# A walk over chunk states placed between the first score maxima of an attention stage, and a last layer mixed from its first latent tile

## The chip, the cores and the metric

The kernel runs on one core of a Trainium2 chip. The metric is the time of one execution in microseconds, measured on the device; before the change it is 6207.06 us, the median of 3 runs (6197.98 to 6211.08). A core has five engines, each with its own instruction queue, that meet only in semaphores: TensorE (PE, matmuls into PSUM; PEld are its weight loads), VectorE (DVE), ScalarE (ACT), GpSimd (POOL) and SyncE (SP, which here only issues DMAs). PSUM has eight banks of 512 float32 columns.

## The reference

Two layers over 2304 tokens of width 1024: 256 context tokens and 2048 latent ones. Each layer projects to the inputs of four groups of heads and sums what they give through one output projection.

```python
def hybrid_layer(x, ctx, ..., ctx_out):
    h_lat = rmsnorm(x, norm_g) * (1.0 + scale[:, None]) + shift[:, None]
    h_ctx = rmsnorm(ctx, norm_g) * (1.0 + scale_c) + shift_c
    s_lat = split_cols(h_lat @ w_in)
    s_ctx = split_cols(h_ctx @ w_in)
    branches = (mlstm_branch(...), diff_attn_branch(...), ssd_branch(...), hgrn2_branch(...))
    y_lat = jnp.concatenate([br[0] for br in branches], axis=-1) @ w_out
    x = x + gate[:, None] * y_lat
...
def bidirectional(run, ctx_fwd, lat_fwd, ctx_bwd, lat_bwd, s0, ctx_out):
    yc_f, sc_f = run(ctx_fwd, s0, ctx_out)
    yl_f, _ = run(lat_fwd, sc_f, True)
    yc_b, sc_b = run(flip(ctx_bwd), s0, ctx_out)
    yl_b, _ = run(flip(lat_bwd), sc_b, True)
...
def chunk_state_scan(decay, incr, s0):
    def step(s, inp):
        d, u = inp
        return d * s + u, s
...
def diff_attend(q, k, v, lam):
    s = jnp.einsum('bqhmd,bkhmd->bhmqk', q, k).astype(F32) * (DA_QK ** -0.5)
    p = jax.nn.softmax(s, axis=-1)
    w = p[:, :, 0] - lam * p[:, :, 1]
    return jnp.einsum('bhqk,bkhv->bqhv', w, v)
```

Three of the four groups (mLSTM, SSD, HGRN2) are linear recurrences in both directions: over chunks a state is decayed and an increment of keys and values added, the context first, then the latent tokens. The fourth is differential softmax attention with its two maps for each of four heads. In the last layer nothing is given out for context tokens (`ctx_out` is false).

## The kernel before

The 2304 tokens are 18 tiles of 128, tiles 0 and 1 the context. The program is a row of stages, and each stage is a block that ends in a barrier of all engines (`k.clear`, with the semaphores cleared). A layer is projection, `gates`, `states`, `mixing`, `attention`, `output`.

`states` walks over the tiles in the order of the backward direction (1, 0, 17, ..., 3, so 17 steps) and writes for each tile the state at which it begins (`k.st`), a tile of 128 x 514: mLSTM, HGRN2, SSD. For a step, SP loads six pieces of the tile into one of four sets of buffers; TensorE makes the running sums of HGRN2's log decays (L1254, L1256), ACT their exponentials (L1235, L1236), VectorE the scaled key (L1183), GpSimd two more scaled operands (L1170, L1171), TensorE the increments (L1266 to L1273), and VectorE new state = decay x old state + increment (L1196 to L1206, reading PSUM). ACT's queue stores the state.

`mixing` goes through the 18 tiles forwards. It makes and keeps the forward state itself and loads the backward one from `k.st`. Its eight sub-steps a tile bind TensorE, ACT, VectorE and GpSimd closely together.

`attention` holds the queries and keys of all tiles, transposed (`QK`), in SBUF, and goes through the queries in groups of four tiles and two halves of heads. The softmax needs each row's maximum first. While one half's probabilities are made, the maxima of the next are made beside them; only for the first half is nothing there to hide them, and they stand by themselves at the start: 40 jobs (`prologue`), each one pair of score matmuls on TensorE (L2295) into one of three pairs of PSUM banks (`PRO`) and one VectorE reduction (L2148), with the key transposes (L2285) between them as the keys are needed. Then `maxima(0)` (L2141) gives the shift, GpSimd cuts it into pieces (`pieces(0)`), and the main loop starts.

All orders are the orders in which the code emits instructions; there is no scheduler. A wait holds up everything behind it on its engine. `Turns` keeps for each PSUM bank a list of the jobs that use it: `take` waits until the job before it in that bank was released.

Of the kernel before, what the change touches and what calls it, by code (L numbers as in the profile page):

```python
# [26 lines left out]
P = 128  # L27
# [8 lines left out]
H = 4  # L36
# [1029 lines left out]
class Turns:  # L1066


    def __init__(self, k, c, uses):
# [5 lines left out]
        self.full = {b: k.sem(c, f"bank{b}_full") for b in self.count}  # L1075
        self.free = {b: k.sem(c, f"bank{b}_free") for b in self.count}
# [29 lines left out]
def states(k, l):  # L1106

    nc = k.nc
    d = 1
    TILES = [*range(CT - 1, -1, -1), *range(NT - 1, CT - 1, -1)]  # L1110
    IN, RING, NLOAD = 4, 4, 6
    with ExitStack() as c:
        key = [k.sb(c, f"key{b}", [P, 256]) for b in range(IN)]
        va = [k.sb(c, f"va{b}", [P, H, 65]) for b in range(IN)]
        fi = [k.sb(c, f"fi{b}", [P, 512]) for b in range(IN)]
        kk = [k.sb(c, f"kk{b}", [P, 256]) for b in range(IN)]
        gt = [k.sb(c, f"gt{b}", [P, GW]) for b in range(IN)]
        xb = [k.sb(c, f"xb{b}", [P, 512]) for b in range(IN)]
        eh = [k.sb(c, f"eh{b}", [P, 256]) for b in range(2)]
        gh = [k.sb(c, f"gh{b}", [P, 2]) for b in range(2)]  # L1120
        kp = [k.sb(c, f"kp{b}", [P, 256]) for b in range(2)]
        xw = [k.sb(c, f"xw{b}", [P, 256]) for b in range(2)]
        kh = [k.sb(c, f"kh{b}", [P, 256]) for b in range(2)]
        S = [k.sb(c, f"S{b}", [P, STW]) for b in range(RING)]
        ones = k.sb(c, "ones", [P, 1])
        tri = k.sb(c, "tri", [P, 4, P])
        s = k.sems(c, "consts_in memsets exps_done weighted keyed updated "
                      + " ".join(f"in{b}" for b in range(IN)) + " " + " ".join(f"st_stored{b}" for b in range(RING)))
        steps = range(NT - 1)
        bk = Turns(k, c, [(("sum", n), n % 2) for n in steps] + [(("ml_hg", n), 2 + n % 2) for n in steps]  # L1130
                   + [(("ss", n), 4 + n % 2) for n in steps])
        h4 = lambda a: a.rearrange("p (h w) -> p h w", h=H)

        def loaded(eng, n):
            eng.wait_ge(s[f"in{n % IN}"], 16 * NLOAD * (n // IN + 1))

        with nc.Block() as block:
            @block.sync
            def _(sp):
                sp.dma_start(tri[:], k.x["c_tri"]).then_inc(s["consts_in"], 16)  # L1140
                sp.wait_ge(s["memsets"], 1)
                for n in steps:
                    b, u = n % IN, k.u[TILES[n]]
                    if n >= IN:
                        bk.wait(sp, ("ml_hg", n - IN))
                        bk.wait(sp, ("ss", n - IN))
                        sp.wait_ge(s["weighted"], n - IN + 1)
                        sp.wait_ge(s["updated"], n - IN + 1)
                    for o, i in ((fi[b][:], u[:, OFF["hg_f"] + 256:OFF["hg_f"] + 768]),
                                 (gt[b][:], k.gt[TILES[n]]),  # L1150
                                 (key[b][:], u[:, 256:512]),
                                 (xb[b][:], k.xc[TILES[n], :, 0:512]),
                                 (kk[b][:], u[:, OFF["hg_k"] + 256:OFF["hg_k"] + 512]),
                                 (va[b][:, :, 0:64], u[:, 512:768].rearrange("p (h w) -> p h w", h=H))):
                        sp.dma_start(o, i).then_inc(s[f"in{b}"], 16)

            @block.gpsimd
            def _(gp):
                gp.memset(ones[:], 1.0)
                for b in range(IN):  # L1160
                    gp.memset(va[b][:, :, 64:65], 1.0)
                gp.memset(S[0][:], 0.0).then_inc(s["memsets"], 1)
                for n in steps:
                    b = n % IN
                    g = lambda name: gt[b][:, GC[name] + 4 * d:GC[name] + 4 * d + 4].unsqueeze(2).to_broadcast([P, H, DH])
                    loaded(gp, n)
                    if n >= 2:
                        bk.wait(gp, ("ml_hg", n - 2))
                        bk.wait(gp, ("ss", n - 2))
                    nc.gpsimd.tensor_tensor(h4(kp[n % 2][:]), h4(key[b][:]), g("wk"), ALU.mult)  # L1170
                    nc.gpsimd.tensor_tensor(h4(xw[n % 2][:]), h4(xb[b][:, 0:256]), g("ws"), ALU.mult) \  # L1171
                        .then_inc(s["weighted"], 1)

            @block.vector
            def _(dve):
                V = nc.vector

                def keyed(n):
                    loaded(dve, n)
                    dve.wait_ge(s["exps_done"], n + 1)  # L1180
                    if n >= 2:
                        bk.wait(dve, ("ml_hg", n - 2))
                    V.tensor_tensor(kh[n % 2][:], kk[n % IN][:], eh[n % 2][:], ALU.mult).then_inc(s["keyed"], 1)  # L1183

                def update(n):
                    old, new, g = S[n % RING], S[(n + 1) % RING], gt[n % IN]
                    if n:
                        dve.wait_ge(s["updated"], n)
                    if n + 1 >= RING:
                        dve.wait_ge(s[f"st_stored{(n + 1) % RING}"], 16 * ((n + 1) // RING))  # L1190
                    bk.wait(dve, ("ml_hg", n))
                    inc = bk[("ml_hg", n)]
                    for p in range(2):
                        sl = slice(p * 65, p * 65 + 65)
                        a = GC["as"] + 2 * d + p
                        V.scalar_tensor_tensor(new[:, sl], old[:, sl], g[:, a:a + 1], inc[:, sl], ALU.mult, ALU.add)  # L1196
                        sl = slice(ST_HG + p * 64, ST_HG + p * 64 + 64)
                        ins = V.scalar_tensor_tensor(new[:, sl], old[:, sl], gh[n % 2][:, p:p + 1], inc[:, sl],
                                                     ALU.mult, ALU.add)
                    bk.release(ins, ("ml_hg", n))  # L1200
                    bk.wait(dve, ("ss", n))
                    inc = bk[("ss", n)]
                    for h in range(H):
                        sl = slice(ST_SS + h * 64, ST_SS + h * 64 + 64)
                        a = GC["ea"] + 4 * d + h
                        ins = V.scalar_tensor_tensor(new[:, sl], old[:, sl], g[:, a:a + 1], inc[:, h * 64:h * 64 + 64],  # L1206
                                                     ALU.mult, ALU.add)
                    bk.release(ins, ("ss", n))
                    bk.freed(dve, ("ss", n))
                    dve.sem_inc(s["updated"], 1)  # L1210

                dve.wait_ge(s["memsets"], 1)
                for n in steps:
                    keyed(n)
                    if n:
                        update(n - 1)
                update(NT - 2)

            @block.scalar
            def _(act):  # L1220
                act.preload_act_table_set(TABLES)

                def store(n):
                    if n:
                        act.wait_ge(s["updated"], n)
                    act.dma_start(k.st[TILES[n]], S[n % RING][:]).then_inc(s[f"st_stored{n % RING}"], 16)

                act.wait_ge(s["memsets"], 1)
                for n in steps:
                    bk.wait(act, ("sum", n))  # L1230
                    if n >= 2:
                        act.wait_ge(s["keyed"], n - 1)
                        act.wait_ge(s["updated"], n - 1)
                    b = bk[("sum", n)]
                    nc.scalar.activation(eh[n % 2][:], b[:, 0:256], ACT.Exp)  # L1235
                    bk.release(nc.scalar.activation(gh[n % 2][:], b[:, 256:258], ACT.Exp), ("sum", n))  # L1236
                    bk.freed(act, ("sum", n))
                    act.sem_inc(s["exps_done"], 1)
                    if n >= 1:
                        store(n - 1)  # L1240
# [1365 lines left out]
```

## Time and profile before

| | |
|---|---|
| median of 3 runs | 6207.06 us |
| the profiled execution: time, span | 6209.43 us, 6207.8 us |
| mean granted clock of TensorE | 0.939 |
| busy: PE, DVE, ACT, POOL | 89%, 47%, 27%, 38% |
| `states`, layer 0 and layer 1 | 87.65 us, 87.07 us |
| start of `attention` to the first shift, both layers | 60.69 us, 60.97 us |

The span runs from the first to the last instruction. Timelines give for a line its start, its duration, the engine, the line of the code, what it writes and reads, how many such instructions are merged (xN), and in brackets how long the engine had been idle and what released it. `SPq` and `ACTq` are DMA issues. The duration of a DMA issue is that of the issue, not of the transfer. The borders in the last two rows are read from the first GpSimd memset of a stage to that of the next, and to the reduction L2141.

### The profile page before, as it was taken

To read this page: it belongs to the slowest core of one execution; us is meant where nothing else is said; L and a number is where in the kernel's file an instruction comes from. 1 tells how busy PE (TensorE), PEld (TensorE's weight loads), DVE (VectorE), ACT (ScalarE), POOL (GpSimd) and SP (SyncE) were. 2 spreads that over 40 slices of the span, in tenths; PEclk is the share of its full clock that TensorE was granted. 3 is DMA by queue.
4 is the path that set the end of the run, shared out by engine and by line. 5 is a ranking of instruction groups with operands and counts; after the bars stand their busy time and mean duration, and the time that the engine had idled before them with its cause. 6 is when DMAs were issued, how large, how long until landed. Compare 5 with 4: busy or idle time off the path is not lost. (4 is left out here: it accounts for less than half of the span.)

```text
span 6207.8 us, 76211 instructions
## 1 busy us (share of the span) xinstructions
PE 5515.7 (89%) x26532; PEld 2933.7 (47%) x26532; DVE 2911.4 (47%) x5007; ACT 1697.7 (27%) x4109; POOL 2329.4 (38%) x1718
## 2 busy tenths in 40 slices
PE   3999999967888799997979999998588877999979
PEld 1444444446666433332435454544466663333334
DVE  0354444444666555551114545455365665555312
ACT  0112111112333234444012121211133332444421
POOL 0111212123333279997001212112233332999920
PEclk7999999977999889998989999999599997999989
DMA  8223233245222100001523333333622211000032
GB/s 293 76 98 103 97 103 100 95 144 160 77 75 91 62 1 8 8 6 53 207 105 103 99 100 101 101 101 108 188 94 74 78 56 56 1 8 8 4 115 88
DMA packets 382933, 534.46 MB, mean 86 GB/s; under 512 B 114784, under 2 KB 263344, under 8 KB 375964
## 3 DMA queue, kind: packets, MB, share of 16 engines
q1 hardware_dynamic: 356124, 455.81, 22.4%
q10 hardware_dynamic: 20448, 41.46, 1.7%
q0 software_dynamic: 6048, 33.11, 1.5%
q8 instruction: 185, 3.03, 0.2%
q14 instruction: 128, 1.05, 0.1%
HBM read 374.82 MB, written 155.13 MB: 85 GB/s over the span
## 5 line engine op out<-in xcount | busy, mean ns | idle before, releaser
L586 PE MATMUL psum<-group_W,projection_hT 128*128 128x512 f32 (+4 forms) x5016 | 1952.7, 546 | 5.9 <-DVE projection_hT L699 5.7
L586 PEld LDWEIGHTS psum<-group_W,projection_hT 128*128 128x128 f32 x5016 | 951.1, 191 | 970.6 <-issue 929.8
L2113 POOL TENSOR_TENSOR attention_PS<-attention_PS 128x1024 f32<-128x1024 f32 x548 | 1265.6, 2354 | 82.0 <-ACT attention_PS L2246 74.7
L2159 DVE TENSOR_REDUCE attention_mxp<-psum 128x1 f32<-128x512 f32 (+1 forms) x1016 | 654.7, 686 | 541.5 <-PE psum L2295 541.5
L2246 ACT ACTIVATE attention_PS<-psum 128x512 f32<-128x512 f32 (+1 forms) x1168 | 630.6, 592 | 717.8 <-PE psum L2349 695.2
L441 POOL TENSOR_TENSOR projection_cx<-projection_cx,projection_cw 128x768 f32<-128x768 f32 x102 | 187.6, 1840 | 1686.9 <-DMA projection_cw<-in_ss_conv_w 1686.9
L2295 PE MATMUL psum<-attention_QK 32*128 32x512 f32 (+1 forms) x2592 | 771.0, 609 | 9.1 <-DVE attention_mxp L2148 6.1
L2343 PE MATMUL psum<-attention_QK 32*128 32x512 f32 x2336 | 665.1, 643 | 0.0
L2361 PE MATMUL psum<-attention_PS,attention_va 128*64 128x512 f32 x2336 | 628.1, 616 | 0.0
L650 ACT ACTIVATE projection_ut<-psum 128x256 f32<-128x256 f32 (+2 forms) x322 | 127.3, 406 | 1420.5 <-PE psum L586 1411.5
L2479 PE MATMUL psum<-output_W,output_yT 128*128 128x512 f32 x1088 | 476.9, 597 | 21.0 <-DMA output_W<-in_w_out 21.0
L752 DVE TENSOR_SCALAR projection_e<-projection_e 128x256 f32<-128x256 f32 (+1 forms) x170 | 58.8, 346 | 849.9 <-ACT projection_e L662 849.8
L2343 PEld LDWEIGHTS psum<-attention_QK 32*128 32x128 f32 x2336 | 181.5, 185 | 444.7 <-issue 400.1
L1448 POOL TENSOR_TENSOR mixing_Xk<-mixing_E,mixing_hkT 128x256 f32<-128x256 f32 x252 | 202.3, 803 | 369.8 <-ACT mixing_E L1514 369.8
L2295 PEld LDWEIGHTS psum<-attention_QK 32*128 32x128 f32 x2592 | 304.0, 189 | 75.6 <-DVE attention_mxp L2148 42.7
L2479 PEld LDWEIGHTS psum<-output_W,output_yT 128*128 128x128 f32 x1088 | 206.2, 192 | 267.7 <-issue 246.0
L1792 PE MATMUL psum<-mixing_mats,mixing_hg 128*128 128x128 f32 x2016 | 312.9, 302 | 0.0
L1626 DVE COPY_PREDICATED mixing_Aw<-mixing_masks,psum 128x512 f32<-128x512 int32 x288 | 210.4, 731 | 181.5 <-PE psum L1805 181.5
L586 PE MATMUL psum<-projection_W,projection_hT 128*128 128x512 f32 (+3 forms) x712 | 295.0, 537 | 0.0
L756 DVE RECIPROCAL projection_e<-projection_e 128x256 f32<-128x256 f32 (+1 forms) x136 | 292.8, 2153 | 4.7
L1514 ACT ACTIVATE mixing_E<-psum 128x512 f32<-128x512 f32 x252 | 150.5, 597 | 498.1 <-PE psum L1792 431.6
L2361 PEld LDWEIGHTS psum<-attention_PS,attention_va 128*64 128x64 f32 x2336 | 116.0, 135 | 354.4 <-issue 325.1
(340 smaller groups left out, 6316.4 us busy)
## 6 DMA issues: line engine op xcount, KB each, us to landing
u<-projection_ut SPq DMA_DIRECT2D x240, 256.0 KB, 2.0
projection_cx<-xbc SPq DMA_DIRECT2D x306, 128.0 KB, 2.2
projection_cw<-in_ss_conv_w SPq DMA_DIRECT2D x102, 384.0 KB, 4.6
mixing_hg<-u SPq DMA_DIRECT2D x36, 1024.0 KB, 5.1
modulation_wm<-in_w_mod SPq DMA_DIRECT2D x12, 2048.0 KB, 8.8
group_W<-in_w_in SPq DMA_DIRECT2D x8, 2316.0 KB, 34.3
output_y<-y SPq DMA_DIRECT2D x34, 512.0 KB, 4.6
group_W<-in_w_in POOLq DMA_DIRECT2D x6, 2316.0 KB, 28.9
```

The lines of the kernel that those rows point to most:

```text
L586: ins = nc.tensor.matmul(ps[n % RING][:, lo - c0:lo - c0 + w], hT[b][:, q], W[q][:, lo:lo + w], start=(q == 0), stop=(q == KT - 1))
L756: st.then(nc.vector.reciprocal(eb, eb))
L1448: G.tensor_tensor(skew(Xk[v % 2][:], 0, [[w, 2], [2 * w, P // w], [1, w]]), skew(E[v % 2][:], 0, [[256 + w, 2], [2 * w, P // w], [1, w]]), ...
L1626: ins = V.copy_predicated(Aw[t % 2][:], m.unsqueeze(1).unsqueeze(1).to_broadcast([P, 2, 2, P]), pair(("A", t, v), 256).rearrange("p x (a i ...
L1792: ins = T(bk[job][:, i * P:(i + 1) * P], hcol(t, "hg_f", i * P, P), m, start=True, stop=True)
L2113: G.tensor_tensor(SA[x % 2][:, rs, 0:w], one[:, rs, 0:w], PT[i % PTB][:, rs, 0:w], ALU.add) \
L2159: bk.release(V.tensor_reduce(mxp[x % 2][:, q:q + nn, 2 * pr + j, a], bk[job, j][:, 0:nn * (hi - lo)].rearrange("p (q n) -> p q n", q=nn), ...
L2246: bk.release(A(PT[i % PTB][:, r, 0:w], bk["st", i, r][:, 0:w], ACT.Exp, scale=scale), ("st", i, r))
L2295: return T(out[:, at:at + hi - lo], QK[rows(r), a0, t * P:(t + 1) * P], QK[rows(r), 2 + a0, lo:hi], start=True, stop=True)
L2343: T(o_, QK[rows(r), 2 + a0, kt * P:(kt + 1) * P], QK[rows(r), a0, t0 * P:(t0 + nq) * P], start=True, stop=False)
L2361: ins = T(k.bank[4 + j][64 * m:64 * m + 64, 0:w], va[:, kts[n], 2 * halves[x][1] + j], PT[i % PTB][:, r, 0:w], start=(n == 0), stop=(n == ...
L2479: ins = nc.tensor.matmul(bk["o", n, a][:], yT[n % 2][:, q], W[:, q, a * 512:(a + 1) * 512], start=(q == 0), stop=(q == KT - 1))
```

## The change

The function `states` is gone. Its walk is in `attention`, which now comes before `mixing`:

```diff
-            stages.append([(f"gates{l}", gates, (l,)), (f"states{l}", states, (l,)), (f"mixing{l}", mixing, (l,)),
-                           (f"attention{l}", attention, (l,))])
+            stages.append([(f"gates{l}", gates, (l,)), (f"attention{l}", attention, (l,)), (f"mixing{l}", mixing, (l,))])
```

In `attention` (new lines): the walk, its buffers, and how the 40 jobs are dealt out over its steps.

```diff
-PRO = (0, 2, 6)
+PRO = (0, 2)
...
+    ahead = CT if l == DEPTH - 1 else 0
+    WALK = [(0, t) for t in range(ahead)] + [(1, t) for t in (*range(CT - 1, -1, -1), *range(NT - 1, CT - 1, -1))]
+    WIN, RING, NLOAD = 3, 4, 7
+    walk = range(len(WALK) - 1)
+    end_walk = len(walk)
...
+    beside = [[m for m in range(len(prologue)) if m * end_walk // len(prologue) == n] for n in walk]
...
+        wk = Turns(k, c, [(("sum", n), 4) for n in walk] + [(("ml_hg", n), 5 + n % 2) for n in walk]
+                   + [(("ss", n), 7) for n in walk], "walk")
...
+                def walk_in(n):
+                    b, (d, t) = n % WIN, WALK[n]
+                    u = k.u[t]
+                    for o_, i in ((fi[b][:, 0:256], u[:, OFF["hg_f"] + d * 256:OFF["hg_f"] + d * 256 + 256]),
+                                  (fi[b][:, 256:512], u[:, OFF["hg_i"]:OFF["hg_i"] + 256]),
+                                  (gt[b][:], k.gt[t]),
+                                  (key[b][:], u[:, 256:512]),
+                                  (xcb[b][:], k.xc[t, :, 0:512]),
+                                  (kk[b][:], u[:, OFF["hg_k"] + d * 256:OFF["hg_k"] + d * 256 + 256]),
+                                  (vx[b][:, :, 0:64], u[:, 512:768].rearrange("p (h w) -> p h w", h=H))):
+                        sp.dma_start(o_, i).then_inc(w_[f"in{b}"], 16)
...
+                for n in walk[WIN:]:
+                    wk.wait(sp, ("ml_hg", n - WIN))
+                    wk.wait(sp, ("ss", n - WIN))
+                    sp.wait_ge(w_["weighted"], n - WIN + 1)
+                    sp.wait_ge(w_["updated"], n - WIN + 1)
+                    walk_in(n)
```

The loops of VectorE and TensorE over it; `keyed`, `update`, `decays` and `increments` hold the instructions of the old stage, `first_maximum` those of the old prologue.

```diff
+                for n in walk:
+                    keyed(n)
+                    for m in beside[n]:
+                        first_maximum(m)
+                    if n:
+                        update(n - 1)
+                update(end_walk - 1)
...
+                keys(range(NT))
...
+                decays(0)
...
+                for n in walk:
+                    if n + 1 < end_walk:
+                        decays(n + 1)
+                    for m in beside[n]:
+                        first_maximum(m)
+                    increments(n)
```

On GpSimd all steps' operands come first, then `pieces(0)`, then the two `gate` products that stood ahead of it. The values `va` are loaded by 4 DMAs in place of 18. In the last layer two steps of the forward direction over the context go ahead of the walk, their end is stored as `k.st[0]`, the backward part starts again from zeros, and mixing skips the context:

```diff
+    skipped = CT if l == DEPTH - 1 else 0
+    count = NT - skipped
+    TILES = range(count)
...
+                if skipped:
+                    sp.dma_start(S[0][:, 0], k.st[0]).then_inc(s["consts_in"], 16)
```

TensorE in layer 0, before: the third step of the states stage. Names are stage, layer, tile and buffer number; the running sums read `fi` and `tri`, the increments `va`/`kp` and `fi`/`kh` and `xw`/`xb`.

```order
L1254 MATMUL psum<-states0_fi2,states0_tri 128x256 [waits states0_bank0_free,states0_in2]
L1256 MATMUL psum<-states0_ones,states0_fi2 128x1 x2
L1266 MATMUL psum<-states0_va1,states0_kp1 64x65 [waits states0_keyed,states0_weighted]
L1268 MATMUL psum<-states0_fi1,states0_kh1 64x64
...
L1273 MATMUL psum<-states0_xw1,states0_xb1 128x128 x2
L1254 MATMUL psum<-states0_fi3,states0_tri 128x256 [waits states0_bank1_free,states0_in3]
```

The same place now, in attention. `QK` are the score pairs whose maxima VectorE takes.

```order
L2285 MATMUL psum<-attention0_fi2,attention0_tri 128x256 [waits attention0_walk4_free,attention0_in2]
L2287 MATMUL psum<-attention0_ones,attention0_fi2 128x1 x2
L2270 MATMUL psum<-attention0_QK 128x512 [waits attention0_pro_read]
L2270 MATMUL psum<-attention0_QK 128x512
...
L2297 MATMUL psum<-attention0_vx1,attention0_kp1 64x65 [waits attention0_keyed,attention0_weighted]
L2299 MATMUL psum<-attention0_fi1,attention0_kh1 64x64
...
L2304 MATMUL psum<-attention0_xw1,attention0_xcb1 128x128 [waits attention0_walk7_free]
L2304 MATMUL psum<-attention0_xw1,attention0_xcb1 128x128
L2285 MATMUL psum<-attention0_fi0,attention0_tri 128x256 [waits attention0_walk4_free,attention0_in0]
```

The running sums of a step now have one bank (4) in place of two, the SSD increments one (7), and the score pairs of the step before stand behind the running sums and their wait for the loads of `fi0`, the fourth tile.

VectorE now, the third and fourth step: `kh` is the scaled key, `mxp` the first maxima, `S` the state.

```order
L2049 TENSOR_TENSOR attention0_kh0<-attention0_kk2,attention0_eh0 128x256 [waits attention0_walk7_free,attention0_walk5_full,attention0_exps_done,attention0_in2]
L2085 TENSOR_REDUCE attention0_mxp0<-psum 128x2 [waits attention0_pro_mm] x3
L2064 SCALAR_TENSOR_TENSOR attention0_S2<-attention0_S1,attention0_gt1,psum 128x65 [waits attention0_walk6_full,attention0_updated]
...
L2074 SCALAR_TENSOR_TENSOR attention0_S2<-attention0_S1,attention0_gt1,psum 128x64 x3
L2049 TENSOR_TENSOR attention0_kh1<-attention0_kk0,attention0_eh1 128x256 [waits attention0_walk7_free,attention0_walk6_full,attention0_exps_done,attention0_in0]
L2085 TENSOR_REDUCE attention0_mxp0<-psum 128x2 [waits attention0_pro_mm] x2
L2064 SCALAR_TENSOR_TENSOR attention0_S3<-attention0_S2,attention0_gt2,psum 128x65 [waits attention0_walk5_full,attention0_updated]
```

Before, the scaled keys and updates followed each other in the states stage, and the 40 reductions stood in one row in attention; now two or three of these stand ahead of each update.

## Rows read from the trace of the kernel before

**Rows 1.** Timeline, layer 0: start us, us, engine line op; borders of the stages.

```profile
1355.32 0.10 POOL L1159 MEMSET states_ones<- 128x1 f32 x1 [42.88 <-POOLq L181]
...
1442.97 0.10 POOL L1430 MEMSET mixing_eps<- 128x1 f32 x1 [12.39 <-POOLq L181]
...
2120.93 0.10 POOL L2060 MEMSET attention_eps<- 128x1 f32 x1 [6.75 <-POOLq L181]
...
2181.62 0.23 DVE L2141 TENSOR_REDUCE attention_mneg<-attention_mxp 128x16 f32<-128x80 f32 x1
```

**Rows 2.** Timeline, layer 1: the same borders.

```profile
4386.61 0.10 POOL L1159 MEMSET states_ones<- 128x1 f32 x1 [42.80 <-POOLq L181]
...
4473.68 0.10 POOL L1430 MEMSET mixing_eps<- 128x1 f32 x1 [11.15 <-POOLq L181]
...
5151.38 0.10 POOL L2060 MEMSET attention_eps<- 128x1 f32 x1 [6.46 <-POOLq L181]
...
5212.35 0.24 DVE L2141 TENSOR_REDUCE attention_mneg<-attention_mxp 128x16 f32<-128x80 f32 x1
```

**Rows 3.** Windows: stretch, length, busy PE PEld DVE ACT POOL, PEclk, DMA, GB/s.

```profile
1355.30:1443.00 87.70, 62.52 (x442) 54.59 (x442) 35.74 (x153) 8.91 (x36) 20.83 (x41) 0.58 0.86 244
2121.00:2182.00 61.00, 47.61 (x234) 21.16 (x236) 42.79 (x47) 11.31 (x20) 5.44 (x7) 0.86 0.38 135
1380.00:1400.00 20.00, 18.10 (x110) 15.28 (x111) 10.19 (x44) 1.79 (x8) 5.32 (x10) 0.50 1.04 281
```

**Rows 4.** Timeline, layer 0: first maxima, and a pair just behind them.

```profile
2136.03 1.99 PE L2295 MATMUL psum<-attention_QK 32*128 32x512 f32 x12
...
2137.21 9.14 DVE L2148 TENSOR_REDUCE attention_mxp<-psum 128x2 f32<-128x1024 f32 x8 [10.66 <-PE psum L2295]
...
2181.74 2.07 PE L2295 MATMUL psum<-attention_QK 32*128 32x512 f32 x4 [0.89 <-DVE attention_mxp L2148]
...
2183.81 1.29 DVE L2159 TENSOR_REDUCE attention_mxp<-psum 128x1 f32<-128x512 f32 x2 [1.96 <-PE psum L2295]
```

**Rows 5.** Timeline, mixing of layer 1: first and last of 18.

```profile
4499.80 0.69 DVE L1653 TENSOR_TENSOR mixing_Xc<-mixing_Ec,mixing_hqT 128x512 f32<-128x512 f32 x1
...
5101.36 0.68 DVE L1653 TENSOR_TENSOR mixing_Xc<-mixing_Ec,mixing_hqT 128x512 f32<-128x512 f32 x1
```

**Rows 6.** Tile states_va: all 34 loads, from issue to landing.

```profile
DMA to landing us min/median/max: 3.5/4.9/6.6
```

**Rows 7.** Timeline, states of layer 0: ACT's hand-over and an update.

```profile
1373.82 0.38 ACT L1235 ACTIVATE states_eh<-psum 128x256 f32<-128x256 f32 x1 [2.51 <-DVEq L1210]
...
1374.40 0.42 DVE L1183 TENSOR_TENSOR states_kh<-states_kk,states_eh 128x256 f32<-128x256 f32 x1 [0.76 <-ACTq L1238]
...
1374.74 0.28 DVE L1196 SCALAR_TENSOR_TENSOR states_S<-states_S,states_gt,psum 128x65 f32<-128x65 f32 x1
...
1375.51 0.85 DVE L1206 SCALAR_TENSOR_TENSOR states_S<-states_S,states_gt,psum 128x64 f32<-128x64 f32 x4
```

**Rows 8.** Timeline, states of layer 0: update to load, running sums to increments.

```profile
1420.60 0.85 DVE L1206 SCALAR_TENSOR_TENSOR states_S<-states_S,states_gt,psum 128x64 f32<-128x64 f32 x4 [0.20 <-PE psum L1273]
...
1421.60 0.33 SPq L1155 DMA_DIRECT2D states_fi<-u  x1
...
1429.38 1.22 PE L1254 MATMUL psum<-states_fi,states_tri 128*128 128x256 f32 x2 [1.28 <-DMA states_va<-u]
...
1431.17 0.49 PE L1266 MATMUL psum<-states_va,states_kp 128*64 128x65 f32 x4
```

**Rows 9.** Timeline, states of layer 0: first and sixth load, their first user.

```profile
1356.03 0.33 SPq L1155 DMA_DIRECT2D states_fi<-u  x1
...
1358.30 0.43 SPq L1155 DMA_DIRECT2D states_va<-u  x1
...
1362.03 0.61 POOL L1170 TENSOR_TENSOR states_kp<-states_key,states_gt 128x256 f32<-128x256 f32 x1 [6.03 <-DMA states_va<-u]
```

**Rows 10.** Tile attention_PS (queries and keys as loaded), layer 0: issue to landing.

```profile
DMA to landing us min/median/max: 12.2/13.2/14.3
```

More of the change, by code:

```diff
@@ L1074, in __init__ @@
             self.nth[job] = self.count[b] = self.count.get(b, 0) + 1
-        self.full = {b: k.sem(c, f"bank{b}_full") for b in self.count}
-        self.free = {b: k.sem(c, f"bank{b}_free") for b in self.count}
+        self.full = {b: k.sem(c, f"{name}{b}_full") for b in self.count}
+        self.free = {b: k.sem(c, f"{name}{b}_free") for b in self.count}
     def __getitem__(self, job):
@@ L2059, in _ @@
                 st = Steps(gp, s["pool_step"])
+                for b in range(WIN):
+                    gp.memset(vx[b][:, :, 64:65], 1.0)
+                gp.memset(zeros[:], 0.0)
+                gp.memset(S[0][:], 0.0).then_inc(w_["walk_sets"], 1)
                 gp.memset(eps[:], EPS)
@@ L2221, in _, with stored @@
                     act.wait_ge(s["key_mm"], t + 1)
-                    A(QK[:, :, t * P:(t + 1) * P], k.bank[4 + t % 2][:].rearrange("p (a n) -> p a n", a=4), ACT.Copy) \
+                    A(QK[:, :, t * P:(t + 1) * P], k.bank[t % 2][:].rearrange("p (a n) -> p a n", a=4), ACT.Copy) \
                         .then_inc(s["key_copied"], 1)
+                def stored(n):
+                    if n:
+                        act.wait_ge(w_["updated"], n)
+                    if n < ahead or (ahead and n > ahead and WALK[n][1] < CT):
+                        act.sem_inc(w_[f"st_stored{n % RING}"], 16)
+                    elif n == ahead and ahead:
+                        act.dma_start(k.st[0], S[n % RING][:]).then_inc(w_[f"st_stored{n % RING}"], 16)
+                    else:
+                        act.dma_start(k.st[WALK[n][1]], S[n % RING][:]).then_inc(w_[f"st_stored{n % RING}"], 16)
+                act.wait_ge(w_["walk_sets"], 1)
+                for n in walk:
+                    wk.wait(act, ("sum", n))
+                    if n >= 2:
+                        act.wait_ge(w_["keyed"], n - 1)
+                        act.wait_ge(w_["updated"], n - 1)
+                    b = wk[("sum", n)]
+                    A(eh[n % 2][:], b[:, 0:256], ACT.Exp)
+                    wk.release(A(gh[n % 2][:], b[:, 256:258], ACT.Exp), ("sum", n))
+                    wk.freed(act, ("sum", n))
+                    act.sem_inc(w_["exps_done"], 1)
+                    if n >= 1:
+                        stored(n - 1)
+                stored(end_walk - 1)
+                stored(end_walk)
                 def turned(x):
@@ L2296, in scored, with first_maximum @@
                              start=True, stop=True)
-                made = CT + QG
-                keys(range(made))
-                for n, (q, a, pr) in enumerate(prologue):
-                    if q == 0 and pr == 0:
-                        ahead = min(NT, groups[0][3][a][1] // P + 4)
-                        keys(range(made, ahead))
-                        made = max(made, ahead)
-                        pe.wait_ge(s["key_copied"], max(CT + QG, groups[0][3][a][1] // P))
-                    if n >= 3:
-                        pe.wait_ge(s["pro_read"], n - 2)
+                def first_maximum(m):
+                    q, a, pr = prologue[m]
+                    if m >= 2:
+                        pe.wait_ge(s["pro_read"], m - 1)
@@ L2308, in _, with decays @@
                     for j in range(2):
-                        ins = scored(k.bank[PRO[n % 3] + j], 0, q, a, 2 * pr + j)
+                        ins = scored(k.bank[PRO[m % 2] + j], 0, q, a, 2 * pr + j)
                     ins.then_inc(s["pro_mm"], 1)
+                def decays(n):
+                    walked(pe, n)
+                    wk.take(pe, ("sum", n))
+                    b, lf = wk[("sum", n)], fi[n % WIN]
+                    T(b[:, 0:256], tri[:, 2 + WALK[n][0]], lf[:, 0:256], start=True, stop=True)
+                    for p in range(2):
+                        ins = T(b[:, 256 + p:257 + p], lf[:, p * P:(p + 1) * P], ones[:, 0:1], start=True, stop=True)
+                    wk.done(ins, ("sum", n))
```

336 lines of the change are left out of this document (135 added, 201 removed).

## The prediction

> **What bounds the kernel now.** I read the stage borders first, since every stage ends in a barrier of all engines and so each stage's time adds to the span. In layer 0 the states stage takes from the first GpSimd memset at 1355.32 to that of mixing at 1442.97, 87.7 us, and the opening of attention, up to the reduction that turns the first maxima into one shift, from 2120.93 to 2181.62, 60.7 us [rows 1]. In layer 1 they are 87.1 and 61.0 us [rows 2]. So the two stretches that the change merges cost 148.4 and 148.1 us, 4.8% of the span.
>
> The windows say what they are made of [rows 3]. The states stage moves 244 GB/s with the DMA engines 86% busy, 281 GB/s in its middle, and its TensorE runs at a granted clock near 0.5 of full, the lower level of 1.2 GHz, though it is counted busy for most of that window. The opening of attention has little DMA (38%), its clock is mostly the upper level (0.86 over the window), and it goes at VectorE's pace: a row of eight first maxima in 9.14 us, 1.13 us each, 1.22 for a single one (a difference of overlap), the 40 of them and the waits for keys in 44.4 us from the first of these at 2137.21 to 2181.62 [rows 1, 4]. Neither engine set is full in both, so on busy shares alone they look made to lie beside each other. Whether they do is decided by waits.
>
> **The change part by part.** (1) The states stage goes in both layers: 87.7 + 87.1 = 174.8 us less, its barrier included.
>
> (2) The last layer's mixing handles 16 tiles and not 18. Its pitch is read from one instruction a tile: first at 4499.80, last of 18 at 5101.36, 601.6/17 = 35.4 us [rows 5]. Two tiles are 70.8 us less. The one new load (the forward state at tile 0) lies beside the eight loads of constants and I cost it at nothing; uncovered it would be one trip of a load, once, 3.5 to 6.6 us [rows 6].
>
> (3) The walk over the tiles is now inside the opening of attention: 17 steps in layer 0, 19 in layer 1 (the two context tiles of the forward direction come first). Its work on VectorE is small: 0.43 for the key product, 1.62 us from the first update (1374.74) to the end of the last four (1375.51 + 0.85) [rows 7]. What matters is the wait that closes a loop. The names of the code: walk_in(n) are tile n's seven loads on SP, decays(n) TensorE's running sums for it, first_maximum its pairs of scores, update(n) VectorE's new state. TensorE's order puts decays(n) ahead of the score pairs of step n-1; these are ahead of update(n-2) on VectorE; and SP, which has three sets of buffers, may issue walk_in(n+1) only when update(n-2) is done. So update(n-3) releases walk_in(n), that releases decays(n), that the pairs of step n-1, these update(n-2): one turn of the loop for each step, and every turn holds a whole trip of the loads. Before, with four sets and no maxima on the way, such a trip had three steps to run in. Queued behind decays(n) on TensorE are the pairs and increments; behind the maxima on VectorE the update; and ACT's exponentials wait for that update.
>
> One turn, at the lower clock:
> - update done to SP's next load: 1420.60 + 0.85 to 1421.60, 0.15 us [rows 8].
> - the loads: last of six issued 2.27 us after the first, and used 3.73 us after that, 6.0 in all [rows 9]; the seventh adds one issue pitch, 0.47 us. The state's own store (257 KB, at the 281 GB/s of [rows 3] 0.9 us) shares the engines; I take half of it. 6.9 us. Bounds for the last load's trip are the least and the greatest landing of this tile's loads, 3.5 and 6.6 us [rows 6]: 6.2 to 9.3 us for the set.
> - decays: 1429.38 to 1431.17, 1.79 us [rows 8].
> - the first pair, 1.2 GHz: 2181.74 to 2183.81, 2.07 us; then two maxima 1.13 + 1.22: 4.4 us. A step with three has only two pairs of banks, so the third pair starts after the first read: 2.07 + 1.22 + 0.1 + 2.07 + 1.22 = 6.7 us [rows 4].
> - update: 1.62 us.
>
> Sum: 14.9 us with two maxima, 17.2 with three. 40 jobs over 17 steps put three into 5 of the 14 steps that are in the loop, over 19 steps into 1 of 16. Six of the last eight jobs, 256 wide, fall into the loop too and save about 0.7 us each. Layer 0: 5 x 17.2 + 9 x 14.9 - 4 = 216 us; layer 1: 17.2 + 15 x 14.9 - 4 = 237 us.
>
> Ahead of the loop: queries and keys land 12.2 to 14.3 us after their issue [rows 10], so until about 17 us after the stage's start; the three first sets (936 KB each, 3.2 us at such a rate) follow to 27 us; then decays, five maxima and the first update: 38 us. Behind it: two updates that wait for nothing loaded, 8 us. The opening becomes 38 + 216 + 8 = 262 us in layer 0 and 283 in layer 1, against 60.7 and 61.0: +201 and +222.
>
> (4) 4 larger loads of the values in place of 18, and the z gates moved behind the walk and behind pieces(0) on GpSimd: nothing, for after pieces(0) GpSimd is wanted only when two steps of scores have been made into exponentials; uncovered they would be two of its products a layer. The keys all made at the start: inside the 38 us. Attention ahead of mixing: the same barriers in another order, nothing.
>
> Sum: -174.8 - 70.8 + 201 + 222 = +178 us. On the profiled execution's 6209.4 us that is 6387; the median shown lies 2.4 us below it, so 6385.
>
> On the loads, the Trainium skill (DMA: Bandwidth & Descriptors, Anatomy of one DMA) fits one transfer of the GpSimd path as about 2.0 us plus its bytes at 436 GB/s. The seventh load would then land 2.3 us after its issue, the set would take 5.0 us and not 6.9, and the sum would be 57 us less, 6328. The trace has no landing of this tile's loads below 3.5 us [rows 6], so it does not agree, and the row is used.
>
> **The clock.** TensorE works for about 7 of a turn's 15 us and waits for the rest. In the window 1380 to 1400, where it had more to do, it was granted 0.50 [rows 3]; I take that level. At the upper level decays are about 0.9 and a pair 1.18 (2136.03 to 2137.21) [rows 4], so a turn is 13.1 or 14.4 us: 24 x 1.8 + 6 x 2.8 = 60 us less over the 30 turns, 6325.
>
> **The rivals.**
> - Loads off the loop, TensorE's single bank for the running sums on it. decays(n) also needs the exponentials of step n-1 to have freed bank 4, and these wait for the same update. For it: this wait has the same distance of one. Against it: it runs beside the 6.9 us of loads and takes far less, ACT's two activations and their hand-over some 0.85 us [rows 7]. A turn would be 8.7 or 11.0 us, 30 x 6.2 = 186 us under the forecast: 6199, no change.
> - Faster: VectorE sets the pace. If the loads of a step were there before it begins, a step would cost VectorE 0.43 + 1.62 and the 0.76 us that it waits for ACT [rows 7] beside its maxima: 17 x 2.8 + 44.4 + 25 until the first tile = 117 us against 148.4, and 123 against 148.1; with mixing -31 - 25 - 71 = -127, 6080. For it: both stretches have room on every engine [rows 3]. Against it: the three sets and the order above. It decides when a turn is below 15.1 - 178/30 = 9.2 us. The Trainium skill (Perfetto Trace Analysis, Optimization Strategy) has a rule behind it: work with different regimes may gain from being interleaved. The shares of [rows 3] agree with it, and the time it would give is this rival's.
> - Slower still: the last load of every set needs the longest trip seen, 6.6 us. 30 x 2.4 = 73 us more, 6458. For it: the store and other loads in flight; against: a lone set leaves the queues empty.
>
> **How the numbers follow.** The loop over the loads gets 0.90: at the lower clock 0.62, the upper clock 0.14, the long trip 0.14. The bank's loop 0.03, VectorE's pace 0.05, the rest for what I have not seen. Median case 6385. The low end of 6295 takes in the upper clock with the 3.5 us landing (60 + 20 less gives 6305), the high end of 6450 most of the long trip; the two rivals at 6199 and 6080 stay out. Faster by over 0.2% (12 us, about what a measurement of this kernel can tell from no change): 0.06; within it: 0.03; slower: 0.91.
>
> **What would show it.** The new trace should have one set of seven loads about every 15 us in the opening, starting right behind an update; TensorE's running sum released by the load of vx; VectorE idle 8 to 9 us ahead of each group of two or three maxima, put down to TensorE; the first shift 262 and 283 us after the start of attention; a low granted clock there; mixing of the last layer near 607 us; no states stage. I am wrong if the sets of loads follow each other in less than 9 us, or if the releaser of the running sum is ACT, or if the rest of attention or mixing changes its pitch.

## The result, and the profile after

The changed kernel takes 6394.66 us (median of 4 runs, 6389.73 to 6399.91) against 6204.52 (4 runs, 6197.98 to 6211.08): a ratio of 1.0307, interval 1.0289 to 1.0324. The profiled execution took 6392.08 us with a span of 6390.4, 182.6 more than the one of before.

Timeline after, the borders that answer to [rows 1, 2] (start us, us, engine line op; L2041 is the first shift):

```profile
1351.16 0.17 POOL L1945 MEMSET attention_vx<- 128x4 f32 x3 [42.30 <-POOLq L181]
...
1615.40 0.24 DVE L2041 TENSOR_REDUCE attention_mneg<-attention_mxp 128x16 f32<-128x80 f32 x1
...
2365.66 0.10 POOL L1253 MEMSET mixing_eps<- 128x1 f32 x1 [7.28 <-POOLq L181]
...
4497.77 0.17 POOL L1945 MEMSET attention_vx<- 128x4 f32 x3 [42.93 <-POOLq L181]
...
4781.93 0.24 DVE L2041 TENSOR_REDUCE attention_mneg<-attention_mxp 128x16 f32<-128x80 f32 x1 [0.50 <-DVE attention_S L2074]
...
5515.30 0.10 POOL L1253 MEMSET mixing_eps<- 128x1 f32 x1 [8.11 <-POOLq L181]
...
6126.61 0.10 POOL L2471 MEMSET output_eps<- 128x1 f32 x1 [6.75 <-POOLq L181]
```

From such borders the span is accounted for. An opening is the stretch from a stage's first memset to the first shift:

| | before | after | difference |
|---|---|---|---|
| states, both layers | 87.65 + 87.07 | none | -174.7 |
| opening of attention, layer 0 | 60.69 | 264.24 | +203.5 |
| opening of attention, layer 1 | 60.97 | 284.16 | +223.2 |
| mixing, layer 1 | 677.70 | 611.31 | -66.4 |
| mixing, layer 0 | 677.96 | 674.63 | -3.3 |
| rest of attention, both | 1480.1 | 1483.6 | +3.5 |
| all else | | | -3.2 |

The openings hold more than the whole difference. The lines below are one turn of the loop in layer 0, that is, the time from one state update to the next; they answer to [rows 7 to 9]:

```profile
1403.31 0.85 DVE L2074 SCALAR_TENSOR_TENSOR attention_S<-attention_S,attention_gt,psum 128x64 f32<-128x64 f32 x4
...
1404.30 0.80 SPq L1908 DMA_DIRECT2D attention_fi<-u  x2
...
1407.14 0.52 SPq L1908 DMA_DIRECT2D attention_vx<-u  x1
...
1411.36 1.22 PE L2285 MATMUL psum<-attention_fi,attention_tri 128*128 128x256 f32 x2 [5.92 <-DMA attention_vx<-u]
...
1413.15 2.09 PE L2270 MATMUL psum<-attention_QK 32*128 32x512 f32 x8
...
1415.28 2.36 DVE L2085 TENSOR_REDUCE attention_mxp<-psum 128x2 f32<-128x1024 f32 x2 [9.94 <-PE psum L2270]
...
1417.55 0.27 DVE L2064 SCALAR_TENSOR_TENSOR attention_S<-attention_S,attention_gt,psum 128x65 f32<-128x65 f32 x1
```

Read it as a ring. The update's end (1404.16) frees a set of buffers. SP issues the seven loads, the last at 1407.14, and that one releases the running sum at 1411.36, 7.06 us after the first issue. The score pairs follow 1.79 us later, and VectorE's maxima have waited 9.94 us for them. The next update begins 4.40 us behind the pairs' start, 15.01 us after the one before (1402.54). The groups of instructions, 1355 to 1650 us (busy, mean ns, idle before and what ended it):

```profile
L2085 DVE TENSOR_REDUCE attention_mxp<-psum 128x2 f32<-128x1024 f32 (+1 forms) x40 | 43.2, 1115 | 151.8 <-PE psum L2270 151.7
...
L2285 PE MATMUL psum<-attention_fi,attention_tri 128*128 128x256 f32 x34 | 19.0, 657 | 90.3 <-DMA attention_vx<-u 89.6 <-ACT attention_gh L2190 0.7
```

VectorE's idle time (151.8 us) is put down to TensorE, and only TensorE's own row (90.3 us) names the load: from the maxima's row alone one would look for the cause in the scores. The windows answer to [rows 3] (length, busy PE PEld DVE ACT POOL, PEclk, DMA, GB/s); the tile's landing, below it, to [rows 6]:

```profile
1386.00:1490.00 104.00, 41.72 (x216) 25.38 (x216) 29.15 (x72) 3.13 (x14) 7.10 (x12) 0.52 0.32 82
```

```profile
DMA to landing us min/median/max: 2.9/4.5/7.9
```

TensorE is busy for 40% of it, VectorE for 28%, the DMA engines for 32%, at a mean granted clock of 0.52. Nothing is full, everything waits in turn.

### The profile page after: what moved, and what is told of

Same layout as the page of the kernel before. It is cut to its first block and busy times, and to the rows that moved or that the text cites. A ratio compares the mean times of both kernels' runs of the same rounds, so it can differ in the third digit from the quotient of the medians.

```text
span 6390.4 us, 74955 instructions
## 1 busy us (share of the span) xinstructions
PE 5475.4 (86%) x26062; PEld 2886.6 (45%) x26096; DVE 2869.2 (45%) x4931; ACT 1672.2 (26%) x4029; POOL 2305.9 (36%) x1687
## 5 line engine op out<-in xcount | busy, mean ns | idle before, releaser
L1618 PE MATMUL psum<-mixing_mats,mixing_hg 128*128 128x128 f32 x1904 | 294.6, 301 | 0.0
```

Source lines behind the costliest of these rows:

```text
L1618: ins = T(bk[job][:, i * P:(i + 1) * P], hcol(t, "hg_f", i * P, P), m, start=True, stop=True)
```

## The experiments

All were timed against the kernel before. 24 steps with two maxima and 6 with three are in the loop of both layers together; the openings are those of layer 0 and layer 1, read from one profiled execution each, while the medians are of 4 to 10 runs.

| kernel | median us | ratio to before, interval | openings us |
|---|---|---|---|
| changed | 6394.7 | 1.0307, 1.0289 to 1.0324 | 264.2, 284.2 |
| six_loads | 6384.2 | 1.0280, 1.0266 to 1.0294 | 257.3, 276.5 |
| apart | 6226.4 | 1.0031, 1.0019 to 1.0043 | 185.9, 192.8 |
| late | 6198.3 | 0.9981, 0.9972 to 0.9990 | 169.2, 180.4 |
| sets4 | 6194.5 | 0.9980, 0.9971 to 0.9989 | 172.3, 176.7 |
| sets3_tight_first | 6178.3 | 0.9950, 0.9933 to 0.9967 | 163.3, 173.2 |
| sets4_late | 6144.9 | 0.9900, 0.9881 to 0.9919 | 148.1, 154.6 |
| skip_only | 6141.2 | 0.9890, 0.9872 to 0.9908 | - |
| sets4_tight_first | 6100.2 | 0.9822, 0.9806 to 0.9839 | 121.0, 133.3 |
| sets6_tight_first | 6089.8 | 0.9809, 0.9784 to 0.9834 | 118.7, 121.0 |

**sets4.** The fourth set lies in rows of `PS` that the attention does not use yet.

```diff
-    WIN, RING, NLOAD = 3, 4, 7
+    WIN, RING, NLOAD = 4, 4, 7
...
+        for lo in (18, 0, 4)[:WIN - 3]:
+            f_ = PS[:, lo:lo + 4].rearrange("p a n -> p (a n)")
+            for sets, a, b in ((key, 0, 256), (fi, 256, 768), (kk, 768, 1024), (xcb, 1024, 1536), (gt, 1536, 1536 + GW)):
+                sets.append(f_[:, a:b])
...
```

> A fourth set of buffers for the walk, nothing else changed. Theory (the turn of the loop holds a whole trip of the seven loads because the sets allow a distance of one step): the distance becomes two, so the loads leave the loop and the wait for bank 4 and ACT's exponentials is next, 8.7 us a turn with two maxima and 11.0 with three, in place of 14.9 and 17.2. 30 turns less 6.2 us each: 6392 - 186 = 6206 us, first shifts about 170 and 190 us after the start of attention. Rival (bank 4 and the hand-over to ACT already set the turn of 15 us, the loads only fill it): no change, 6390 us, turns stay at 15. Rival (traffic: the loads take the time they take whatever the distance, 7 us a set one after the other plus nothing hidden): turns near 9 to 10 us, 6230 us or more, and VectorE still put down to loads.

Measured 6194.5, with openings of 172.3 and 176.7 us for the expected 170 and 190. The timeline, one turn:

```profile
1407.77 0.27 DVE L2069 SCALAR_TENSOR_TENSOR attention_S<-attention_S,attention_gt,psum 128x65 f32<-128x65 f32 x1
...
1409.44 1.22 PE L2309 MATMUL psum<-attention_xw,attention_PS 128*128 128x128 f32 x4 [2.86 <-DVE attention_S L2079]
...
1409.57 0.38 ACT L2194 ACTIVATE attention_eh<-psum 128x256 f32<-128x256 f32 x1 [8.27 <-DVEq L2083]
...
1410.46 1.06 PE L2290 MATMUL psum<-attention_fi,attention_tri 128*128 128x256 f32 x2
...
1412.09 2.09 PE L2275 MATMUL psum<-attention_QK 32*128 32x512 f32 x8
...
1414.21 2.36 DVE L2090 TENSOR_REDUCE attention_mxp<-psum 128x2 f32<-128x1024 f32 x2 [3.64 <-PE psum L2275]
...
1416.49 0.28 DVE L2069 SCALAR_TENSOR_TENSOR attention_S<-attention_S,attention_PS,psum 128x65 f32<-128x65 f32 x1
```

Update to update is 8.72 us; from the update at 1416.49 to the next at 1427.48, with three maxima, 10.99. The running sum waits for no load, so the loads were the wait, and one set more takes them off the loop. The turns are those that the prediction's first rival priced at 8.7 and 11.0 by the wait for bank 4. But the trace puts TensorE's idle time elsewhere. It idles ahead of the SSD increments (L2309), until the update frees bank 7: 27.0 us between 1395 and 1500, against none ahead of the sums. The sums stand right behind these increments; bank 4 comes free at nearly the same time, from ACT's last exponential at 1409.85. The last turns, with 256-wide maxima, take 6.8 us, four of them in layer 1, and some others there 8.3; that is why its opening is shorter than expected.

**late.** Three sets, another order on TensorE.

```diff
                 for n in walk:
-                    if n + 1 < end_walk:
-                        decays(n + 1)
                     for m in beside[n]:
                         first_maximum(m)
+                    if n + 1 < end_walk:
+                        decays(n + 1)
                     increments(n)
```

> Three sets as they are; TensorE issues the running sums of step n+1 behind the score pairs of step n instead of ahead of them. Theory (what closes the loop at distance one is TensorE's order: pairs behind a running sum that waits for loads): the maxima no longer wait for loads, the loop over the loads now runs update(n-3), loads 6.9, running sums 1.79, increments about 1, update 1.62 = 11.5 us for two steps, 5.7 a step, and TensorE's own work at 1.2 GHz is next, two pairs 4.1 + 1.8 + 1.5 = 7.4 us (8.8 with three): 6392 - 24 x 7.5 - 6 x 8.4 = about 6160 us (6130 to 6210), the first shift about 145 us after the start in layer 0. Rival (the trip of the loads itself is exposed each step whatever the order): 6390 us, turns of 15 us. Rival (bank 4 and ACT): 6390 too, with ACT named as what releases the running sums.

6198.3: the order alone removes as much as the fourth set does, but 38 us less than I expected.

```profile
1424.60 0.85 DVE L2074 SCALAR_TENSOR_TENSOR attention_S<-attention_S,attention_gt,psum 128x64 f32<-128x64 f32 x4
...
1432.79 1.22 PE L2285 MATMUL psum<-attention_fi,attention_tri 128*128 128x256 f32 x2 [4.04 <-DMA attention_vx<-u]
...
1436.85 2.09 PE L2270 MATMUL psum<-attention_QK 32*128 32x512 f32 x8
...
1441.25 0.28 DVE L2064 SCALAR_TENSOR_TENSOR attention_S<-attention_S,attention_gt,psum 128x65 f32<-128x65 f32 x1
```

My loop ended at the increments. But on TensorE the next pairs stand behind these, and on VectorE their maxima ahead of the update: from the first update's start (1423.84) to the one at 1441.25 it is 17.4 us for two steps, 8.7 a step and not 5.7. The trip got longer when its distance grew.

**six_loads.** One load for two neighbouring pieces in the backward steps.

```diff
+                    for o_, i in ([(fi[b][:], u[:, OFF["hg_f"] + 256:OFF["hg_f"] + 768])] if d else
+                                 [(fi[b][:, 0:256], u[:, OFF["hg_f"]:OFF["hg_f"] + 256]),
+                                  (fi[b][:, 256:512], u[:, OFF["hg_i"]:OFF["hg_i"] + 256])]) + [
...
```

> The gate and input columns that lie side by side are fetched by one load for the backward steps (34 of 36), as the old stage did: six loads a set and not seven, the same bytes. Theory (a turn waits for the last load of a set, and SP issues one every 0.47 us): 0.47 us less in each of 30 turns, 14 us, 6378 us, turns of 14.5 to 15. Rival (the bytes or one slow load set the trip, not the number of loads): no change, within 3 us of the changed kernel. Rival (fewer, larger loads land later or earlier than small ones): more than 25 us off in either direction.

The openings are 7.0 and 7.7 us shorter, 14.7 together for the expected 14; of the median 10.4 came through. The intervals of the two ratios overlap, so this rests on the trace: the mean turn fell from 15.8 to 15.3 us in layer 0 and from 15.1 to 14.6 in layer 1, the 0.5 us of one issue. The last load's issue is on the loop.

**apart.** `beside` puts all 40 maxima into the walk's first step.

```diff
-    beside = [[m for m in range(len(prologue)) if m * end_walk // len(prologue) == n] for n in walk]
+    beside = [[m for m in range(len(prologue))] if n == 0 else [] for n in walk]
```

> Attention as changed, but all 40 first maxima stand at the walk's first step, so that the walk behind it has none between its steps. Theory (the maxima are the link that shortens the distance to one): without them update(n-1) is what waits for the loads that update(n-3) released, two steps for 0.15 + 6.9 + 1.8 + 1 + 1.6 = 11.5 us, 5.7 us a step. Opening: about 17 us until queries and keys are there, 46 us of maxima, then 16 or 18 steps of 5.7: 155 us in layer 0 and 167 in layer 1, against 264 and 284: 6392 - 226 = 6166 us (6140 to 6200). So work one behind the other would beat the interleaved form. Rival (each step pays its whole trip of loads, maxima or not): steps of 10.5 us, opening 63 + 16 x 10.5 = 231 and 252 us, 6327 us. Rival (overlap of maxima and walk is worth what it was meant to be, and the time is lost elsewhere): slower than 6392 by up to 40 us a layer, about 6470 us.

6226.4, 168 us under the changed kernel: the work one behind the other beats the interleaved one, so the maxima between the steps are the link that the theory needs. The expected 6166 was missed in two places. The row of maxima took 1379.84 to 1440.31, 60.5 us, where [rows 1, 4] have 44.4, and its reductions stand 0.34 or 0.61 us apart. Two things differ from before: two pairs of banks in place of three, and the clock. TensorE was granted 0.54 from 1380 to 1440 and its score matmuls took 1.06 us (median), against 0.96 and 0.59 us in the old row (2137 to 2181). Two reductions follow each other in 3.40 us, which is about one pair at the lower clock (2.07) and one reduction (1.23), that is one trip through a bank. By this estimate it takes both: three pairs of banks at the lower clock would need 1.13 us a reduction, and two at the upper clock (1.18 for a pair) about 1.25, both close to VectorE's own 1.23. No run separates the two. And the walk behind it went at 13 us for two steps:

```profile
1442.97 0.82 SPq L1908 DMA_DIRECT2D attention_fi<-u  x2
...
1446.43 0.86 SPq L1908 DMA_DIRECT2D attention_fi<-u  x2
...
1450.90 1.22 PE L2285 MATMUL psum<-attention_fi,attention_tri 128*128 128x256 f32 x2 [6.63 <-DMA attention_vx<-u]
...
1463.87 1.22 PE L2285 MATMUL psum<-attention_fi,attention_tri 128*128 128x256 f32 x2 [6.23 <-DMA attention_vx<-u]
```

Two sets are issued right behind each other, and the first is used 7.93 us after its issue in place of 7.06.

**skip_only.** The kernel before, with mixing's `count` and `skipped` of the change, and the old stage two steps longer.

```diff
-    TILES = [*range(CT - 1, -1, -1), *range(NT - 1, CT - 1, -1)]
+    ahead = CT if l == DEPTH - 1 else 0
+    WALK = [(0, t) for t in range(ahead)] + [(1, t) for t in (*range(CT - 1, -1, -1), *range(NT - 1, CT - 1, -1))]
...
```

> The kernel before with the change's other part alone: the last layer's mixing begins at the first latent tile, and its old states stage makes the forward context state in two more steps. Theory (the parts add, and this one is worth what the changed trace shows): mixing 611 in place of 678 us, -66, two more steps of the states stage at 4.6 us, +9: 6205 - 57 = 6148 us (6140 to 6156). Rival (mixing's start with a state loaded from memory, or the two forward steps with seven loads, cost more): 6165 or more. Rival (the two tiles are worth their full pitch of 35.4 us each and the two steps hide): 6134.

6141.2. Borders in layer 1:

```profile
4389.25 0.10 POOL L1164 MEMSET states_ones<- 128x1 f32 x1 [43.26 <-POOLq L181]
...
4486.88 0.10 POOL L1447 MEMSET mixing_eps<- 128x1 f32 x1 [11.22 <-POOLq L181]
...
5093.99 0.10 POOL L2080 MEMSET attention_eps<- 128x1 f32 x1 [6.75 <-POOLq L181]
```

The states stage is 97.6 us (+10.6 for two steps), mixing 607.1 (-70.6, the forecast's 70.8). So this half of the change gains 1.1%, and the other half, the walk merged into attention, cost about 250 us (6394.7 against 6141.2).

**sets4_late.** Both edits of above.

> Both single changes together: four sets of buffers, and running sums of step n+1 behind the score pairs of step n. Theory (with loads at distance three and the running sums out of the maxima's way, the next wait is that of the SSD increments for bank 7, which update(n-1) frees): pair 2.1, two maxima 2.36, update 1.62, increments 1.15 = 7.2 us a turn, with three maxima 9.7; against 8.7 and 11.0 with four sets alone: 24 x 1.5 + 6 x 1.3 = 44 us less, 6194 - 44 = 6150 us. Rival (the two fixes remove the same wait, so the second buys nothing): 6194. Rival (the transfers bind, 936 KB a step beside a store): turns not below 8, about 6175.

6144.9: the two edits remove different waits, and in layer 0 a turn is 7.2 us with two maxima and 9.5 with three, as expected. But the whole is no faster than skip_only (6141.2): with openings of 148.1 and 154.6 us, merging takes about as long as the stages that it replaces.

**sets6_tight_first.** Six sets (not shown), and two orders:

```diff
                     wk.done(ins, ("ml_hg", n))
+                    for m in beside[then] if then < end_walk else []:
+                        first_maximum(m)
                     wk.take(pe, ("ss", n))
...
                 for n in walk:
-                    keyed(n)
                     for m in beside[n]:
                         first_maximum(m)
+                    keyed(n)
```

> Six sets of buffers; TensorE issues the score pairs of step n+1 between the two halves of the increments of step n; VectorE takes the maxima of a step ahead of its scaled key, so that they run beside ACT's exponentials. Theory (a chain of waits of distance one sets the turn, and this order leaves: scaled key to increments 1.15, pair 2.1, two maxima 2.36, scaled key 0.43, less what lies beside the update): 6.1 us a turn and 8.4 with three maxima, at TensorE's lower clock: 24 x 2.6 + 6 x 2.6 = 78 us less than with four sets alone, 6116 us. If TensorE is busy enough for the upper clock: 4.7 and 6.5, 6070. Rival (the transfers bind at 281 GB/s, 4.6 us a step, or VectorE does, 4.7 us): 6070 too, with TensorE at the upper clock. Rival (interleaving cannot beat the two stages apart, since the turn never falls under the 9.2 us of the forecast's break-even together with the 71 us of mixing): not under 6150.

6089.8, 0.9809 of before. Its updates, and windows of this kernel and of sets4_late:

```profile
1395.15 0.27 DVE L2077 SCALAR_TENSOR_TENSOR attention_S<-attention_S,attention_gt,psum 128x65 f32<-128x65 f32 x1
...
1399.74 0.28 DVE L2077 SCALAR_TENSOR_TENSOR attention_S<-attention_S,attention_PS,psum 128x65 f32<-128x65 f32 x1
...
1405.78 0.27 DVE L2077 SCALAR_TENSOR_TENSOR attention_S<-attention_S,attention_PS,psum 128x65 f32<-128x65 f32 x1
```

```profile
1386.00:1460.00 74.00, 60.02 (x466) 40.24 (x462) 59.64 (x148) 6.30 (x28) 16.46 (x26) 0.78 0.81 227
```

```profile
1386.00:1490.00 104.00, 82.48 (x470) 50.36 (x467) 62.55 (x158) 6.30 (x28) 15.47 (x26) 0.58 0.66 176
```

The steps shown take 4.59 us with two maxima and 6.04 with three, but the mean over the 30 turns is 5.2. Where the score pairs ran at the lower clock (2.09 us for eight matmuls, as at 1423.65, and not 1.14) a step with two maxima took 5.5 to 6.3 us as well. VectorE is busy for 81% and TensorE was granted 0.78, against 0.58 in sets4_late. The time lies between those expected for the two clocks.

**sets3_tight_first, sets4_tight_first.** The same orders with three and four sets.

> The two new orders of the version with six sets (score pairs between the two halves of the increments, maxima ahead of the scaled key), with the change's own three sets of buffers. Theory (what a step costs is the whole trip from an update over the loads to the next update, divided by the number of steps that the order and the sets let it span): update to load 0.15, loads 7.0, running sums 1.8, first increments 1.15, pair 2.1, two maxima 2.36, scaled key 0.43, update 1.62 = 16.6 us, now over two steps: 8.3 us a step, about 9.5 with three maxima, 6177 us (6165 to 6195), openings near 158 and 172 us. Rival (the order alone is what the six sets' kernel gains from): 6090. Rival (three sets always leave the whole trip in each step): 6390.

> The same orders with four sets. Theory (trip over distance): 16.6 us over three steps, 5.5 us, which is within the 4.7 to 6.1 us that the six sets' trace shows for a step, so the loads are almost out of the way: 6090 to 6105 us, openings near 120 to 127. Rival (a trip grows once two or three sets are in flight, as in the walk without maxima, where the last load came about 8 us after the first's issue): 17.6 over three, 5.9, and threes at 6.5: 6110 to 6120. Rival (six sets are needed, four still pay 8 us a step): 6170.

6178.3 and 6100.2. The whole trip over the number of steps that it may span comes out in both: the mean of the 30 turns is 8.3 us with three sets (16.6/2) and 5.6 with four (16.6/3). With three sets the loads are what is waited for: the running sums stand 23.5 us for them between 1392 and 1470. With four it is 4 us in that stretch of layer 0, so that the loads are only part of what sets the step there. The change's three sets with these orders are 216 us better than the change, a fourth set 78 more, the fifth and sixth 10 (the intervals of the last two overlap; the two openings together are 14.6 us shorter).

## Why the prediction was right

- **Stages gone:** -174.7, as read from the borders.
- **Mixing of the last layer:** -66.4 for -70.8. The pitch over 16 tiles was (6076.3 - 5541.7)/15 = 35.6, not 35.4, which is 3.8 of the 4.4 us; start and end are each within 0.3 us of the old ones. In skip_only the stage was 70.6 us shorter. The same mixing code took 603.0 to 617.6 us in the experiments that have the merged walk, so the stage varies by more than the 4.4 us.
- **The loop:** the ring stands in the trace step by step. Loads 7.06 us for 6.9, running sums 1.79 for 1.79, pairs and maxima 4.40 for 4.4. Turns of two wide maxima were 14.8 to 15.6 us in layer 0 and 13.7 to 16.2 in layer 1 for 14.9, turns of three 17.4 to 18.1 for 17.2. The loop as a whole took 221.4 and 240.9 us for 216 and 237, and the first update was done 35 us after the start for 38: two small errors of opposite sign, so that the openings of 264.2 and 284.2 for 262 and 283 owe a little to luck. One thing to look for was put too low: VectorE was to idle 8 to 9 us ahead of its maxima, while the prediction's own turn leaves 9.7 (14.9 less 1.62, 0.43, 0.76 and 2.36). It idled 8.6 to 11.2 us. That the loads close the loop is shown by sets4, that the order makes it a loop of one step by late and apart, that the issues are in it by six_loads.
- **Lower clock:** the mean granted clock in the loop was 0.52, close to the level of 1.2 GHz that was taken, and eight score matmuls took 2.09 us.
- **Nothing for the order of stages, for 4 value loads and late gates:** rest of attention and mixing of layer 0 together +0.2 us.
- **Rivals:** the first, priced 6199, was next in line by its time, for sets4 gave 6194.5. Its mechanism was not quite the one seen: the wait that shows is that for bank 7, 1.07 us from the update's end to the running sum (1409.39 to 1410.46), where the rival had 0.85 us for ACT's hand-over and bank 4. That the two nearly agree is luck. VectorE's pace was priced 6080 with openings of 117 and 123; sets6_tight_first has 118.7 and 121.0, and 6089.8. The break-even turn of 9.2 us fits sets4: its 30 turns take 127.0 + 133.1 us, 8.7 each, which is 30 x 0.5 = 15 us under break-even, and it measured 13 us under the kernel before. The long trip stayed out: the longest landing of 7.9 us belongs to the sets issued ahead of the loop, and between 1380 and 1600 the last load of a set landed after 3.0 / 4.6 / 4.8 us (min / median / max), not 6.6.
- **The Trainium skill's figure** (DMA: Bandwidth & Descriptors, Anatomy of one DMA), a fit for the GpSimd path of about 2.0 us plus bytes, would have given 6328. The last load, 4.22 us from its issue to the running sum, speaks against it here. The first two loads of a set, of the same 128 KB, landed after a median of 2.3 us in the same stretch: it is the last of seven that takes longer. The Trainium skill's advice (Perfetto Trace Analysis, Optimization Strategy) that interleaving work of different regimes may gain agreed with this case only once the waits were cut: the same merge cost 250 us as written and gained 51 over skip_only with six sets and the other orders.

Sum of the prediction on the profiled execution: +178; measured +182.6.

## What to carry to other kernels

Before two stages are merged because neither fills an engine, walk once around each loop of waits: buffer release, issue, landing, each in-order engine's queue up to the next release. Divide that whole trip by the number of steps that it may span; if the quotient is above what the busiest engine needs for a step, expect it as the time of a step (here 15, 8.7, 8.3 and 7.2 us were met so). Each instruction that is put between two steps can lengthen the trip and shorten the distance at once: here two maxima did both.

## What the runs showed of the hardware

- The same score matmuls ran at the lower clock in the slow loops and in about half of the steps at the upper one in the fast: eight took 2.09 us in the changed kernel's loop, and 1.14 in about half of the steps of sets6_tight_first, whose mean granted clock there was 0.78 against 0.52. So removing waits paid twice: I had expected 6116 at the lower clock and 6070 at the upper, and got 6089.8. In apart TensorE was counted busy for 15.00 of 15.00 us (1395 to 1410) and was granted 0.50, so the counted busy time alone does not tell the clock.
- A set of seven loads took 7.06 us from the first issue to its user with no other set in flight, and 7.93 with a second set issued 3.46 us behind it.
- The mixing stage took 674.6 to 684.3 us in layer 0 and 603.0 to 617.6 in layer 1 over the profiled executions of the changed kernel and the eight experiments on it, with the same code in all nine. A difference of 10 us in one stage is therefore not an effect of an edit elsewhere until something else shows it.
